# One rotary transpose per key block, packed output weights, and second-layer modulation chunks loaded ahead, in a two-layer diffusion trunk kernel

## The reference

```python
mod = (jnp.einsum('bd,de->be', jax.nn.silu(cond), w_mod[i]) + b_mod[i]).reshape(cond.shape[0], N_MOD, D_MODEL)[:, :, None, :]
shift1, scale1, gate1, shift2, scale2, gate2 = (mod[:, j] for j in range(N_MOD))
h = rms_norm(x, norm1_g[i]) * (1 + scale1) + shift1
qs, kv = token_tensors(h, w_in[i], kv_g[i], qn_g[i], kn_g[i], rope)
...
x = x + gate1 * mix(qs, kv_read, w_uk[i], w_uv[i], diff_lambda[i], diff_g[i], lam_init, w_out[i])
h = rms_norm(x, norm2_g[i]) * (1 + scale2) + shift2
x = x + gate2 * hier_moe(h, w_grp[i], b_grp[i], w_rtr[i], b_rtr[i], w_gate[i], w_up[i], w_down[i])
```

```python
k_nope = jnp.einsum('bkr,rhd->bkhd', ckv, w_uk)
k_a = jnp.concatenate([k_nope, jnp.broadcast_to(k_rope[:, :, None, :], (B, Sk, MLA_HEADS, MLA_ROPE))], axis=-1)
```

## Time and profile before

| what | us |
|---|---|
| median of 3 runs | 1419.57 |
| lowest and highest run | 1418.41, 1423.47 |
| the profiled execution: own time | 1415.01 |
| its span in the trace | 1413.3 |
| PE busy in the span | 1254.8 (89%) |
| DVE, ACT, POOL busy | 717.3, 412.3, 212.4 |

### The profile page before, as it was taken

One profiled execution on the slowest core, in us unless ns is written; L12 is line 12 of the kernel. 1 busy time (PEld: TensorE's weight loads), 2 busy tenths in 40 slices (PEclk: granted clock), 3 DMA queues, 4 the chain that ended last, 5 costly groups with the idle time before them and its releaser, 6 DMA issues. The chain is left out here.

```text
span 1413.3 us, 22646 instructions
## 1 busy us (share of the span) xinstructions
PE 1254.8 (89%) x8208; PEld 742.1 (53%) x8208; DVE 717.3 (51%) x1728; ACT 412.3 (29%) x931; POOL 212.4 (15%) x305
## 2 busy tenths in 40 slices
PE   4999999999999869988949999899999994999981
PEld 3455556777766634433425555677776663444330
DVE  0344436777744525553514454466786346455452
ACT  2111145666611201111111111566665010111111
POOL 1210021010021112211111001210101111122202
PEclk9899999999999979999959999999999996999996
DMA  9700288010041797999950004760001324899965
GB/s 349 295 14 1 69 303 226 1 32 16 1 150 75 286 384 257 356 372 350 315 163 18 1 1 168 268 163 1 32 16 64 138 90 163 321 374 377 342 208 181
DMA packets 73708, 245.19 MB, mean 173 GB/s; under 512 B 6072, under 2 KB 14753, under 8 KB 60977
## 3 DMA queue, kind: packets, MB, share of 16 engines
q1 hardware_dynamic: 56080, 183.26, 34.5%
q0 software_dynamic: 17056, 58.61, 14.2%
q10 hardware_dynamic: 432, 1.36, 0.2%
HBM read 213.87 MB, written 31.00 MB: 173 GB/s over the span
## 5 line engine op out<-in xcount | busy, mean ns | idle before, releaser
L1871 PE MATMUL ps<-ring,hT_region 128*128 128x512 f32 (+1 forms) x640 | 271.1, 580 | 3.4 <-ACT hT_region L961 3.4
L1871 PEld LDWEIGHTS ps<-ring,hT_region 128*128 128x128 f32 x640 | 121.1, 193 | 135.0 <-issue 134.4
L1333 DVE TENSOR_SCALAR_CACHE_REDUCE ring<-ps 128x768 f32<-128x768 f32 (+1 forms) x168 | 132.7, 820 | 104.6 <-PE ps L1945 85.0
L1015 ACT ACTIVATE ring<-ring,negm 128x768 f32<-128x768 f32 (+1 forms) x168 | 137.6, 820 | 26.8 <-DVE ring L1333 26.8
L2070 PE MATMUL ps<-ring,hT_region 128*128 128x384 f32 (+1 forms) x480 | 143.5, 454 | 0.0
L2226 PE MATMUL ps<-ring,hT_region 128*128 x272 | 127.5, 624 | 10.5 <-SPq L594 4.5
L1945 PE MATMUL ps<-arena,qT 64*128 64x384 f32 (+1 forms) x640 | 124.8, 507 | 6.2 <-DVE ring L1333 2.9
L2070 PEld LDWEIGHTS ps<-ring,hT_region 128*128 128x128 f32 x480 | 89.2, 190 | 42.9 <-issue 1.5
L1998 PE MATMUL ps<-work,arena 128*64 128x128 f32 x1600 | 105.0, 278 | 5.6 <-ACT work L1031 4.3
L1031 ACT ACTIVATE work<-ps 128x512 f32<-128x512 f32 x128 | 75.8, 592 | 98.1 <-PE ps L1763 98.1
L1998 PEld LDWEIGHTS ps<-work,arena 128*64 128x64 f32 x1600 | 85.9, 136 | 24.6 <-issue 14.3
(11 more groups left out here) (303 smaller groups left out, 1735.0 us busy)
## 6 DMA issues: line engine op xcount, KB each, us to landing
ring<-in_w_mod SPq DMA_DIRECT2D x24, 2048.0 KB, 9.3
ring<-in_moe_w_gate SPq DMA_DIRECT2D x32, 1024.0 KB, 8.9
ring<-in_moe_w_up SPq DMA_DIRECT2D x32, 1024.0 KB, 12.4
arena<-in_moe_w_down SPq DMA_DIRECT2D x32, 1024.0 KB, 14.7
ring<-in_w_in SPq DMA_DIRECT2D x6, 2048.0 KB, 21.1
arena<-mod_rows POOLq DMA_DIRECT2D x12, 512.0 KB, 5.7
x_rows<-x POOLq DMA_DIRECT2D x10, 512.0 KB, 3.0
h_rows<-work POOLq DMA_DIRECT2D x10, 512.0 KB, 2.9
```

The source lines that it names most:

```text
L1015: act.activation(v, v, ACT.Exp, bias=negm[:, 2 * (k % 3) + m:2 * (k % 3) + m + 1], scale=-1.0, accum_out=sums[:, c:c + 1]).then_inc(exp_do ...
L1333: ts(o_, i_, -pair_of(p)[4], None, ALU.mult, ALU.min, accum_out=col).then_inc(m_ready, 1)
L1871: last = mm(ps[:, b, 0:n], hT[:, c, t * P:(t + 1) * P], w[:, c, :], start=(c == 0), stop=(c == KC - 1))
```

## The change

Four things change.

First, the shared rotary part: `keys1` transposes the rotary columns of a unit once, into columns 0 to 127 of bank 7, ahead of its other four transposes; `keys2` loses the three identity matmuls. ACT fills the rotary rows of the three planes with two copies of 32 partitions each, which read the bank once and write three times (`key_copies_a`), and the rows of the heads' own part with two copies of 32 partitions in place of one of 128 (`key_copies_b`). A new semaphore `kr_evac` says that bank 7 is free again: `keys1` of the next unit and `hT_round(t, 0)`, which writes the same bank, wait for it. In layer 1 the first `keys1` also waits until DVE has read the modulation columns in bank 7 (`a1_ready`).

Second, the output weights lie packed in slots 0 and 1 (`WO_AT`, `wo_block`).

Third, modulation chunk 0 of layer 1 goes to slot 2, and is loaded behind the output weights while layer 0's attention runs. Chunk 1 goes to slot 3 and chunks 2 and 3 to a free part of `arena` (`mod_home`), all three when the attention is over.

Fourth, the first four experts: `LATE` is (2, 3, 0, 1), and `first_experts` writes their loads out. In layer 0 gate/up of expert 2 comes first, when the second output block of the last tile is done; gate/up of experts 0 and 1 follow modulation chunks 0 and 1, and down of both follow chunk 2. In layer 1 gate/up of expert 0 is loaded during the attention, and that of expert 1 with both downs when it is over.

Some semaphores are merged in passing (`p_fac`, `f_ss`, `f_rs`), with the same waits under other names.

```diff
+WO_AT = [KC * c0 for c0, _ in WO_COLS]
...
-LATE = (3, 2, 0, 1)
+LATE = (2, 3, 0, 1)
...
-        uses += [("out", l, b, (b + N_MOD - MOD_FIRST) % 3) for b in range(len(WO_COLS))]
+        uses += [("out", l, b, b) for b in range(len(WO_COLS))]
...
-            uses += [("mod", l + 1, j, LATE[j]) for j in range(MOD_FIRST)]
+            uses += [("mod", l + 1, j, (2, 3, 1, 0)[j]) for j in range(MOD_FIRST)]
...
+        def mod_home(l, j):
+
+            if l >= 1 and j in (2, 3):
+                return arena[:, DN0 + 4096 * (3 - j):DN0 + 4096 * (4 - j)]
+            return slot[USES[USE_AT["mod", l, j]][3]]
...
+            def slot_free(kind, l, i):
...
+                elif kind == "mod" and l >= 1:
+                    if i == 0:
+                        sp.wait_ge(mod_done, l * N_MOD - 2)
+                    else:
+                        sp.wait_ge(pv_done, l * NUT)
...
+            def first_experts(l):
+
+                if l + 1 < DEPTH:
+                    at = (l + 1) * N_MOD
+                    sp.wait_ge(wo_done, l * 15 + 3 * (NT - 1) + 2)
+                    gate_up_of(l, 2)
+                    for e in range(2):
+                        sp.wait_ge(mod_done, at + e + 1)
+                        gate_up_of(l, e)
+                    sp.wait_ge(mod_done, at + 3)
+                    for e in range(2):
+                        down_of(l, e)
...
+                for r in (32, 96):
+                    last = act.activation(kT[r:r + 32, 0:3, KCOL[u]:KCOL[u] + P],
+                                          ps[r:r + 32, 7, 0:P].unsqueeze(1).to_broadcast([32, 3, P]), ACT.Copy)
+                last.then_inc(kr_evac, 1)
...
-                act.activation(kT[:, 0:3, KCOL[u]:KCOL[u] + P],
-                               ps[:, 5, 0:384].rearrange("p (j n) -> p j n", j=3), ACT.Copy)
+                for r in (0, 64):
+                    act.activation(kT[r:r + 32, 0:3, KCOL[u]:KCOL[u] + P],
+                                   ps[r:r + 32, 5, 0:384].rearrange("p (j n) -> p j n", j=3), ACT.Copy)
...
                 pe.wait_ge(kA_evac, l * NU + u + 1)
+                pe.wait_ge(kr_evac, l * NU + u)
+                if u == 0 and l >= 1:
+                    pe.wait_ge(a1_ready, l + 1)
+                tr(ps[:, 7, 0:P], kt[:, 128:256])
...
-                    mm(ps[:, 5, j * P:(j + 1) * P], wuk[:, j * P:(j + 1) * P], ckvT[:], start=True, stop=False)
-                    mm(ps[:, 5, j * P:(j + 1) * P], kt[:, 128:256], ident[:], start=False, stop=True)
+                    mm(ps[:, 5, j * P:(j + 1) * P], wuk[:, j * P:(j + 1) * P], ckvT[:], start=True, stop=True)
...
+                    if r == 0:
+                        pe.wait_ge(kr_evac, l * NU + (t + 1 if t or l else 2))
```

More of the change, by code:

```diff
@@ L550, in _ @@
                 sp.dma_start(cond[:, k * KC:(k + 1) * KC], src.rearrange("(p c) -> p c", c=KC)).then_inc(s_cond, 16)
[L552 to L564, removed]
+            def slot_free(kind, l, i):
+                if kind == "in":
+                    sp.wait_ge(mod_done, i + 1)
+                elif kind == "mod" and i >= MOD_FIRST + 3:
+                    sp.wait_ge(mod_done, l * N_MOD + i - 2)
+                elif kind == "mod" and i >= MOD_FIRST:
+                    sp.wait_ge(z_done, l * 4 * NT + 4 * (NT - 1) + i - MOD_FIRST + 1)
+                elif kind == "mod" and l >= 1:
[3 more added lines that the diff above has]
+                        sp.wait_ge(pv_done, l * NUT)
+                    if i != 1:
+                        g = USE_AT["out", l - 1, USES[USE_AT["mod", l, i]][3]]
+                        sp.wait_ge(w_landed[USES[g][3]], USE_CUM[g])
+                elif kind == "out" and i < 2:
+                    sp.wait_ge(mod_done, l * N_MOD + N_MOD - 1 + i)
             def gate_up_weights(l, e, to, landed):
@@ L606, in load_x @@
                     sp.dma_start(x_t[t], x_rows[l][(1 + t) * P:(2 + t) * P, :]).then_inc(s_xin[t], 16)
+            def first_experts(l):
[9 more added lines that the diff above has]
+                        down_of(l, e)
+                else:
+                    sp.wait_ge(mod_done, DEPTH * N_MOD)
+                    gate_up_of(l, 0)
+                    sp.wait_ge(pv_done, (l + 1) * NUT)
+                    down_of(l, 0)
+                    gate_up_of(l, 1)
+                    down_of(l, 1)
+                    sp.wait_ge(wo_done, l * 15 + 3 * (NT - 1) + 2)
+                    gate_up_of(l, 2)
+                sp.wait_ge(experts_ready, l + 1)
+                for e in range(2):
+                    pass_on(gu_loaded, l, e, wgu_landed, 32)
+                    pass_on(dn_loaded, l, e, wd_landed, 16)
+                sp.wait_ge(s_hg[l][0], 16)
+                if l + 1 < DEPTH:
+                    sp.wait_ge(mod_done, (l + 1) * N_MOD + MOD_FIRST)
+                down_of(l, 2)
+                sp.wait_ge(wo_done, l * 15 + 15)
+                gate_up_of(l, 3)
+                down_of(l, 3)
+                for e in range(RING, NE + 2):
+                    if e < NE:
+                        gate_up_of(l, e)
+                    pass_on(gu_loaded, l, e - 2, wgu_landed, 32)
+                    if RING <= e - 1 < NE:
+                        down_of(l, e - 1)
+                    pass_on(dn_loaded, l, e - 2, wd_landed, 16)
             for g, (kind, l, i, at) in enumerate(USES):
@@ L657, in _ @@
                 else:
-                    columns("w_mod", l, i * 512, (i + 1) * 512, to, w_landed[at])
+                    columns("w_mod", l, i * 512, (i + 1) * 512, mod_home(l, i), w_landed[at])
             sp.wait_ge(x_final, DEPTH)
@@ L2060, in out_block @@
                     if t == 0:
-                        w_slots["out", b] = landed("out", b)
+                        landed("out", b)
                     if n >= 4:
```

56 lines of the change are left out of this document (18 added, 38 removed).

## The result

The changed kernel took 1408.64 us, the median of five runs (1405.0 to 1411.67), beside 1419.93 us for the kernel before in the same session. The ratio is 0.9925 (95% interval 0.99 to 0.995), which is 10.6 us less (the two medians lie 11.3 apart); 1409 was forecast. The profiled execution took 1405.0 us, with a span of 1403.2 us.

The account below looks back on a forecast made before the run. PE was taken to bound the input projections, with loads perhaps in the way at layer 0's routing (481 to 512 us). 6.2 + 0.7 + 3.6 = 10.5 us less gave a 1409 us median, range 1405 to 1413 (8 in 10: 1402 to 1416).

Parts of the forecast that it names:

- the two halves: Whole kernel: keys' edit alone 6.9 us less (1412.7), loads' edit alone 3.6 us less (1416).
- Keys, input projections: Input projections, PE: three matmuls fewer, one transpose more per unit, 0.56 us each; 11 units give 6.2 us.
- ACT's copies: Key units, ACT: three more copies of 0.37 us each, 1.1 us per unit, without making PE wait.
- the cover: Input projection: 4.1 us between the rotary copies' end and the next tile's first transpose, which waits for them.
- The new wait: Layer 1's first keys1: waiting for DVE's modulation columns costs nothing, as they are done by 714.3 us.
- Unit 0 of layer 1 and the boundary: Start of layer 1, at half clock: the shorter unit on the path saves 0.7 us, lower end 0.
- Gather: Layer 0's routing: earlier loads leave the first gather freer, so PE starts 3.6 us sooner, ends 0 and 5.1.
- strict order of arrival: Layer 0's first gather: alternative to packet-by-packet queue sharing; gives the later end, 2.8 us gained.
- Nothing further in: Experts after layer 0's gather, and layer 1's gather: no gain expected from earlier loads; weight waits stay near 15 us.
- waits go too: Rival: PE's waits for expert weights vanish as well, up to 14.9 us, giving 1394; chance 0.06.
- The clock: Key units: rival that added transposes lower PE's granted clock, 1.85 us per unit, giving 1435; chance 0.05.
- nothing gained at the gather: Rival at layer 0's gather: loads or stores still in the way, only 6.9 us from keys, 1412.7; chance 0.20.

Follow-up runs that it names:

- b2: Changed kernel plus two tiny two-column matmuls in each of layer 0's seven key units; 1411.55 us, ratio 0.9955.
- c2: Kernel before plus 58 more PE instructions (long-fulfilled waits) at PE's start, moving the experts' code; ratio 1.001.
- b3: Changed kernel plus two tiny two-column matmuls in each of layer 1's seven key units; 1409.45 us, ratio 0.9936.
- a2: The changed kernel run once more, unchanged; 1407.25 us, ratio 0.9925.
- b1: Kernel before plus one PE wait for a1_ready ahead of layer 1's first key transposes; 1419.19 us, ratio 1.0001.
- c1: Changed kernel plus 70 PE instructions (long-fulfilled waits) at the start, putting the experts' code in its old place; 1409.04 us, ratio 0.9948.
- a1: The kernel before run once more, unchanged, for a second profile; 1419.69 us (one run).
- a3: Kernel before with the keys' edit and merged semaphores only, loads as before; 1408.53 us, ratio 0.9947.
- a4: Kernel before with the loads' edit and merged semaphores only, keys as before; 1413.76 us, ratio 0.9977.
- c3: Changed kernel with ACT's four 32-partition copies per key unit split into twelve, one per chunk; 1407.62 us, ratio 0.9935.
- b4: Changed kernel, but layer 0's down weights of experts 0 and 1 are asked for only after the first gather lands; 1404.51 us, ratio 0.9895.
- c4: b4 plus nine unneeded 384-column matmuls per layer in attention tile 0; 1411.82 us, ratio 0.9961.

## Why the prediction was right, step by step

*The total* is right, 1408.64 for 1409, and so are the two halves. It is partly luck: a term of 3.4 us was missing, and other differences covered it.

*Keys, input projections.* Forecast 5 x 0.56 = 2.8 us for layer 0 and, without unit 0, 6 x 0.56 = 3.4 for layer 1. The price per unit is exact: from one unit's transposes to the next's, full steps take 29.49 us in every profile with the old keys and 28.93 in every one with the new, in both layers (padded layers and the last, shorter step left out). In the rows it is 0.67 off and 0.10 on. Layer 0 shows all five, 2.8 us; its first score matmul lies at 200.0 on average in the five profiles with old keys and at 196.8 in the eight with new ones (b2 left out), 3.2 earlier, the rest being starts that scatter. Layer 1 gave 2.4 of the 3.4 (159.6, c2 left out, to 157.2, b3 left out). In five of the eight profiles the stretch from the last unit to the scores stayed at 8.3 us instead of falling to 7.8. And from the first block to the next unit's transposes it took 8.5 to 10.0 us, 9.3 on average, where it had been 8.7. That block starts at half the clock: the clock rose 3.6 us behind its start before, 4.8 in the changed kernel, 5.9 in a2. b2 and b3, which put two matmuls back, took 0.45 of the 0.56 back in their layer.

*ACT's copies* were priced at 0.37 us each and take 0.50; the cover went from 4.1 to 3.7 us. Nobody waited, as forecast.

*The new wait* costs nothing, as forecast: b1.

*Unit 0 of layer 1 and the boundary: this step failed.* The prediction had 0.7 us from a shorter unit on the path. The profiles gave 31.45 - 27.3 = 4.1 us, because the walk became 4 us shorter and the load of x, not unit 0, became the last to arrive. With the code in its old place (c1) it is 31.5 - 30.9 = 0.6 us: the step's working held, its premise "PE comes to this unit at 723.53" did not. I had taken PE's arrival as given by the tiles, and it hangs on where the code lies.

*Gather.* Forecast 3.6 us with ends of 0 and 5.1. The reason given for the middle was too hopeful: the weights of experts 0 and 1 were in at 503.84, not at 500.7, so the gather shared the engines for most of its time. The routing, from output projection to PE's transposes, is 108.9 us in the profiles with the old loads (before, a1, b1 and a3) and 105.6 in after, a2, a4, b2, b3 and c3: 3.3 us. In c1 it was 106.8, with a wait of 7.0 us at the gather; c1 moved the code of this stage too. The landing in the profiled execution, 505.07, is nonetheless at the later end of "between 503.6 and 505.1". The place was right (a4 against a3), and b4 shows that what it took above 4.3 us is sharing. The Trainium skill's rule that a DMA engine goes round its queues packet by packet (DMA: Bandwidth & Descriptors, Queues, rings and completion order) gave 3.6 us, strict order of arrival 2.8; 3.3 tells neither out. The kernel before had settled it already, in its trace:

```profile
486.89 0.45 SPq L573 DMA_DIRECT2D arena<-in_moe_w_down  x1
```

This load landed at 509.54. The gather was issued 12 us behind it, at 499.20 on POOL's queue, and PE worked on it from 507.86. So it did not stand behind all that SP had asked for, and the trace agrees with the rule.

*Nothing further in.* In the first pair of profiles the waits for weights fell from 14.9 to 11.7 us, but in layer 0's experts alone they were 9.0 before and in a1, and 7.3, 9.0, 8.6 and 10.5 in after, a2, b4 and c1. That is scatter; the rival "waits go too" found nothing.

*The clock.* No fall at the five transposes: 0.97 over layer 0's projection as before. The Trainium skill (TensorE: Matmul & The Clock Gate, Part 4: PE-mode transpose) says that the full clock does not engage for transposes; for five of them, with full matmuls around, the trace shows no price. What the clock does cost lies in attention tile 0 and in the first block of layer 1, in both kernels. In layer 1 the stage took 198.5 us on average in the five profiles with old keys and 200.4 in the eight with new ones (c4 aside); whether that is the change's or chance, thirteen executions don't tell.

Summed from the stages, 3.2 + 2.4 + 4.1 + 3.3 = 13.0 us of gain stand against 10.6 measured; attention of layer 1 (+1.9) and of layer 0 (199.6 to 198.8 on average, -0.8) cover 1.1 of the difference, and the other 1.3 us are within what single profiles scatter. The prediction's own range did not follow from its terms: with nothing gained at the gather (1412.7) and 2 us for the median its upper end is 1414.7, not 1413. The result lies far inside either.

## What to carry to other kernels

- In a program with branches on data, the length of straight code ahead of them is a hidden term: taking 70 PE instructions out made an empty stretch about 4 us shorter, and putting 70 empty ones back undid that. Before a few microseconds at such a place are put down to an edit, move the code without changing the work.
- One pair of profiles showed several differences of 1 to 5 us, and two of them were one execution's (the clock in layer 0's attention, the waits for weights). A second profile of each kernel sorts them at once.
- Where a stage repeats one step, read the step, from one unit to the next: here it gave 0.56 us to 0.01, where the stage's length scattered by more than 1 us.
- A filler has the price of a full matmul of its shape: read it from a row first, and compare it with the loss it is to prevent.

## What the runs showed of the hardware

- An f32 matmul of 2 columns with new weights takes 0.18 us until the next starts (0.22 by what two of them add to a unit), one of 128 columns 0.22 to 0.25. Narrower matmuls save little, fewer ones save 0.2 us each.
- ACT copies of 32 partitions from PSUM: 0.50 us for 384 columns, 0.20 for 128, so three small ones cost 0.1 us more than one large.
- PE's walk past three empty tiles took 12.5 to 12.7 us in five executions at one place of the code and 5.9 to 10.7 us in nine at other places.
- The instruction queue brought PE's code in blocks of 16,384 bytes, each 0.9 to 1.1 us in transit in the two walks; two started within the walk of 12.64 us and two within that of 6.79.
- A gather issued on POOL's queue 12 us behind the last of 6.3 MB of loads on SP's was in before that last load (by 507.86 and at 509.54).
- The granted clock fell to half in attention tile 0 for no, one or two stretches per layer, and the stage took from 197.2 to 202.3 us. It is not all that two executions differ by: the first two profiles of the kernel before have the same sum of both attention stages (396.1 us) and lie 4.7 us apart.
